# Fused two-layer block on one core: one activation table set named ahead of three norms, and two residual updates kept in PSUM

## The reference, cut to what matters

```
def rmsnorm(x, g):
    return x * lax.rsqrt(jnp.mean(x * x, axis=-1, keepdims=True) + EPS) * g

mix = (g_ssd * y_ssd + g_sc * y_sc) @ w_o                 # o1
x = x + gt1 * rmsnorm(mix, mix_post_g)                    # residual update 1
h = rmsnorm(x, ffn_pre_g) * (1.0 + sc2) + sh2             # feeds w_up (up1)
f = (silu(u_gate) * u_val) @ w_down                       # down1
x = x + gt2 * rmsnorm(f, ffn_post_g)                      # residual update 2
# layer 2
h = rmsnorm(x, attn_norm) * (1.0 + scale_a) + shift_a     # feeds w_in_2 (tok2)
...
x = x + gate_a * ((g_a * o_a + g_b * o_b) @ w_o)          # o2
h = rms_norm(x, ffn_norm) * (1.0 + scale_f) + shift_f     # feeds w_up_2 (up2)
x = x + gate_f * ((silu(gt) * val) @ w_down)              # down2
```

## Time and profile before

| | |
|---|---|
| time, median of 3 runs | 1058.37 us (1056.8 to 1060.44) |
| span of the profiled execution | 1056.5 us |
| PE busy | 1025.1 us, 97% of the span |
| ACT busy | 634.4 us, 60% |
| DVE busy | 556.2 us, 53% |
| POOL busy | 689.8 us, 65% |
| table loads of the preload (L1384) | 5, 1283 ns each |
| table loads between Ln and Exp (L1146) | 5, 1283 ns each |

### The profile page before, as it was taken

How to read it: one execution, slowest core, us unless ns; L and a number is a source line. 1 busy time by engine, 2 the same in 40 slices (tenths; PEclk the granted TensorE clock), 3 DMA queues, 4 the chain that set the end, 5 groups by cost and what they waited for, 6 DMA issues and landing times.

```text
span 1056.5 us, 23232 instructions
## 1 busy us (share of the span) xinstructions
PE 1025.1 (97%) x8537; PEld 966.4 (91%) x8537; DVE 556.2 (53%) x1165; ACT 634.4 (60%) x1133; POOL 689.8 (65%) x306
## 2 busy tenths in 40 slices
PE   7999999999999989999999899999989999999998
PEld 5999999988799979999999799998667699999998
DVE  2577625579874435565522542296566735444400
ACT  4555764477774576666645656744566557666642
POOL 2598899811269855988799287790031075988795
PEclk9999999999999999999999999999999999999999
DMA  9988888655547863777687289865201043665563
GB/s 380 383 306 282 273 307 298 235 191 187 174 146 259 282 236 105 273 235 248 204 279 268 80 283 360 330 239 191 99 21 60 1 140 122 217 193 189 168 217 111
DMA packets 62616, 226.43 MB, mean 214 GB/s; under 512 B 6960, under 2 KB 8272, under 8 KB 61264
## 3 DMA queue, kind: packets, MB, share of 16 engines
q1 hardware_dynamic: 61344, 221.23, 60.5%
q10 hardware_dynamic: 1200, 4.23, 1.4%
HBM read 224.35 MB, written 1.08 MB: 213 GB/s over the span
## 4 chain that ended last, share of the span: by engine, by line
PE 75%; issue 9%; POOL 9%; DVE 3%; ACT 3%; DMA 1%; POOLq 0%; ACTq 0%; DVEq 0%; SPq 0%
PE psL L553 68%; POOL WL L505 8%; PE psO L553 3%; PE psS L553 2%; PE psL L1092 1%; DMA ring<-wts 1%; ACT psL L1685 0%; ACT WH L1155 0%; ACT R L1273 0%; PE psS L1036 0%; ACT L1146 0%; DVE sm L2288 0%; PE psS L1063 0%; PE psS L966 0%; DVE CT L2052 0%
## 5 line engine op out<-in xcount | busy, mean ns | idle before, releaser
L505 POOL TENSOR_TENSOR WL<-ring,WH 128x1024 fp32r<-128x1024 f32 (+1 forms) x282 | 670.4, 2399 | 239.8 <-ACT WH L1155 186.7
L553 PE MATMUL psL<-HR,WH 128*128 128x256 f32 (+1 forms) x3096 | 513.5, 278 | 1.8 <-DVE HR L1796 0.9
L553 PEld LDWEIGHTS psL<-HR,WH 128*128 128x128 f32 (+1 forms) x3096 | 452.6, 187 | 7.5 <-issue 4.8
L553 PE MATMUL psL<-HR,WL 128*128 128x256 f32 x1536 | 396.2, 276 | 0.0
L1155 ACT ACTIVATE WH<-ring 128x1024 fp32r<-128x1024 f32 (+1 forms) x210 | 216.5, 1042 | 107.8 <-PE psL L553 71.9
L553 PEld LDWEIGHTS psL<-HR,WL 128*128 128x128 f32 x1536 | 275.2, 188 | 0.0
L553 PE MATMUL psL<-RR,WH 128*128 128x256 f32 x1356 | 205.2, 277 | 2.4 <-DVE RR L1981 1.2
L553 PEld LDWEIGHTS psL<-RR,WH 128*128 128x128 f32 x1356 | 185.5, 187 | 3.8 <-issue 2.8
L553 PE MATMUL psL<-RR,WL 128*128 128x256 f32 x672 | 145.0, 277 | 0.3 <-POOL WL L505 0.3
L2080 DVE SCALAR_TENSOR_TENSOR CT<-psL,par,CT 128x254 f32<-128x254 f32 (+1 forms) x176 | 80.9, 480 | 107.1 <-ACT CT L1463 102.0
L1454 ACT ACTIVATE WH<-ring 128x1024 fp32r<-128x1024 f32 (+1 forms) x88 | 92.9, 1058 | 71.4 <-PE psL L553 68.0
(11 more groups left out here) (274 smaller groups left out, 1122.8 us busy)
## 6 DMA issues: line engine op xcount, KB each, us to landing
ring<-wts SPq DMA_DIRECT2D x285, 512.0 KB, 4.2
adaring<-ada_w SPq DMA_DIRECT2D x80, 512.0 KB, 4.8
R<-ada_w SPq DMA_DIRECT2D x8, 1024.0 KB, 16.2
ring<-wts SPq DMA_DIRECT2D x16, 384.0 KB, 3.8
R<-cum_dram ACTq DMA_DIRECT2D x8, 512.0 KB, 4.1
R<-wts SPq DMA_DIRECT2D x8, 512.0 KB, 6.4
ring<-wts SPq DMA_DIRECT2D x8, 288.0 KB, 2.8
adaring<-wts SPq DMA_DIRECT2D x4, 512.0 KB, 5.2
```

What stands on the lines that cost most here:

```text
L505: nc.gpsimd.tensor_tensor(WL[:, k, 0:n], ring[:, k, 0:n], WH[:, k, 0:n].bitcast(F32), SUB).then_inc(lo_done, 1)
L553: return nc.tensor.matmul(out, lhsT, rhs, start=start, stop=stop)
```

## The change

`preload` and its five calls go. In their place `roots_table` names one set, `natural_log_exp_and_others`, three times: at the beginning of `scale_and_square` for o1 and for down1, and in the o2 stage at m == 0, behind the first `feed`. The first root of o1 and of down1 is made by `root_in_bank`: Ln goes to `RS` as before, Exp goes back into the bank `psS` from which Ln read. `add_normed` reads the root from that bank and puts the product into a free bank of `psL`, not into `CT`; it gives the bank `psS` free itself at the end. The second roots, and the one after o2, stay as they were, in `RS`.

```
-            def preload():
-
-                st.link(A(sm[:, 94:95], eps_col[:, :], ACT.Ln))
+            def roots_table():
+
+                nc.scalar.preload_act_table_set("natural_log_exp_and_others")
+
+            def root_in_bank(name):
+
+                act.wait_ge(s_done, SCRATCH[name] + 1)
+                st.link(A(RS[:, 0, :], sbank(name)[:, 0:T], ACT.Ln, scale=1.0 / D, bias=eps_col[:, :]))
+                A(sbank(name)[:, 0:T], RS[:, 0, :], ACT.Exp, scale=-0.5).then_inc(rs_ready, 1)
...
                 act.wait_ge(lead_ready, 1)
+                roots_table()
                 for m in range(8):
...
-                    if m == 6:
-                        preload()
...
             def square_x(base, sq_free_after):
 
-                preload()
...
             scale_and_square("o1", MIX, lead[:, 8:16], 0, SQ_O1)
-            stat_root("stat_o1", D, RS[:, 0, :])
+            root_in_bank("stat_o1")
...
             scale_and_square("down1", FO, lead[:, 24:32], 1, SQ_DOWN1)
-            stat_root("stat_down1", D, RS[:, 0, :])
+            root_in_bank("stat_down1")
...
                 square_o2(m)
-                if m == 6:
-                    preload()
+                if m == 0:
+                    roots_table()
...
-            def add_normed(src, rs, x_base):
-
-                def wide(buf, j, n):
-                    return buf[:, j:j + n, :]
-
-                for j, n, slot in ((0, 2, 0), (2, 2, 2), (4, 2, 0), (6, 1, 2), (7, 1, 3)):
-                    t = CT[:, slot:slot + n, :]
+            def add_normed(src, name, u0, x_base):
+
+                rs = sbank(name)[:, 0:T]
+                for i, (j, n) in enumerate(((0, 2), (2, 2), (4, 2), (6, 1), (7, 1))):
+                    t = psL[:, (u0 + 2 + i % 2) % 4, 0:n * T].rearrange("p (a b) -> p a b", b=T)
                     if j >= 4:
-                        dve.wait_ge(x_ready, x_base + j - 2)
-                    st.link(V.tensor_tensor(t, wide(src, j, n), rs.unsqueeze(1).to_broadcast([P, n, T]), MUL))
-                    V.tensor_tensor(wide(X, j, n), wide(X, j, n), t, ADD).then_inc(x_ready, n)
+                        dve.wait_ge(x_ready, x_base + j - (2 if n == 2 or j == 6 else 1))
+                    st.link(V.tensor_tensor(t, src[:, j:j + n, :], rs.unsqueeze(1).to_broadcast([P, n, T]), MUL))
+                    V.tensor_tensor(X[:, j:j + n, :], X[:, j:j + n, :], t, ADD).then_inc(x_ready, n)
+                dve.wait_ge(x_ready, x_base + 8)
+                dve.sem_inc(s_free[SCRATCH[name] % 2], 1)
...
-            add_normed(MIX, RS[:, 0, :], 0)
-            dve.wait_ge(x_ready, 8)
+            add_normed(MIX, "stat_o1", PLAN.at["up1"][1], 0)
...
-            add_normed(FO, RS[:, 0, :], 8)
...
-            dve.wait_ge(x_ready, 16)
+            add_normed(FO, "stat_down1", PLAN.at["tok2"][1], 8)
```

## The result

The changed kernel takes 1052.08 us (median of 4 runs, 1050.98 to 1054.07), the kernel before beside it 1059.12 (4 runs, 1056.8 to 1060.44): ratio 0.994, 95% interval 0.9924 to 0.9956, so 7.0 us faster. The forecast took 6.88 off. The profiled execution took 1054.07 us with a span of 1052.3.

What follows compares the result with a forecast made beforehand. PE was taken to bound the kernel, with ACT's loads counting only in the three norms. 3.41 + 3.40 - 0.56 + 0.63 = 6.88 us off the median 1058.37 gave 1051.5, range 1048.5 to 1055.0.

Steps and rivals of the forecast that it cites:

- o1 to up1: Norm after o1: early load 0.74, first Exp 1.28, DVE's wait for POOL 0.11, second Exp 1.28; gain 3.41 us.
- second Exp with `make_h`: Second root after o1: without its table load Exp comes 1.28 us earlier, and POOL doesn't hold make_h; gain 1.28.
- down1 to tok2: Norm after down1: first Exp 1.28, POOL's wait 0.16, second Exp 1.28, clock 0.68; gain 3.40 us.
- the clock: Sums in down1's norm: one PE idle stretch goes, so the clock stays up; gain 0.68 us, other end 0.
- The loads at down1: Load at down1's beginning delays POOL's split, so PE stands once; cost 0.56 us, between 0 and 1.28.
- o2 to up2: Norm after o2: Exp 1.28 earlier, but POOL's split holds make_h, whose root stays in SBUF; gain 0.63 us.
- rival (3): POOL doesn't hold make_h after o2 and down1 has slack for the load: gain 8.09, 1050.3 us; chance 0.10.
- PSUM operands: DVE operations of the first two norms: cost taken as nothing, 0.16 us at most; 0.78 by the Trainium skill.
- Rival (4): PSUM operands dearer than the 256-wide rows say, by 0.07 each: gain 6.04, 1052.3 us; chance 0.10.
- (5): Layer 2's projections, 635 to 712 us, give back the first two stages' gain: only 0.63 left, 1057.7; chance 0.12.
- (6): The named set isn't honoured and each Ln and Exp gets its own load: 3.4 slower, 1061.8 us; chance 0.05.
- a longer stretch there: Sign that the forecast is wrong: the stretch from 600 to 870 us becomes longer.

Runs made afterwards that it cites:

- before_again: The kernel before, unchanged, run once more for a second profile; 1057.76 us.
- tables_only: Against the kernel before: only the named set replaces the old preloads, roots and products stay in SBUF; 1056.95 us, ratio 0.9972.
- psum_only: Against the changed kernel: the old dummy Ln preloads put back, root and product kept in PSUM; 1057.94 us, ratio 0.9988.
- root_only: Against the changed kernel: the product goes back to CT in SBUF, only the root stays in PSUM; 1054.81 us, one run.
- load_moved: Against the changed kernel: down1's table load placed after unit 4 instead of at the stage's beginning; 1052.49 us, ratio 0.9942.
- two_loads_again: Against the changed kernel: a second table load in front of the one at down1; repetition of the same program's first run; 1053.59 us.
- last_bank: Against the changed kernel: the root after o2 also put into its PSUM bank, read there by make_h; 1051.82 us, ratio 0.9929.
- both: Against the changed kernel: down1's load after unit 4 and the root after o2 in its PSUM bank; 1050.65 us, ratio 0.9926.

## Why the prediction was right

The range held, and its steps can be read off one by one. Milestones count from PE's first `fill` matmul (381.23 and 578.05 before, 380.64 and 576.28 after), in us:

| | before, o1 | after | gain | before, down1 | after | gain |
|---|---|---|---|---|---|---|
| first Ln | 2.78 | 2.03 | 0.75 | 2.15 | 2.04 | 0.11 |
| first Exp | 4.55 | 2.52 | 2.03 | 3.92 | 2.53 | 1.39 |
| first product of DVE | 5.05 | 3.00 | 2.05 | 4.37 | 2.95 | 1.42 |
| second Ln | 12.27 | 10.11 | 2.16 | 12.32 | 10.07 | 2.25 |
| first product of the next stage | 16.19 | 12.67 | 3.52 | 16.44 | 12.82 | 3.62 |

- **o1 to up1, forecast 3.41, measured 3.52.** Early load 0.74 (0.75); first Exp 1.28 (2.03 - 0.75); DVE's wait for POOL 0.11 (2.16 - 2.05); second Exp with `make_h` 1.28, measured 1.36. Of the last 0.08, 0.07 lies between the starts of the second Exp and of `make_h`: 0.52 or 0.53 us in `before`, `before_again` and `tables_only`, 0.45 in `psum_only`, `root_only` and the changed kernel. So it comes with the new `add_normed` and not with the loads; why isn't shown.
- **down1 to tok2, forecast 3.40, measured 3.62.** First Exp 1.28 (1.39 - 0.11); POOL's wait and the clock 0.16 + 0.68 = 0.84, measured 2.25 - 1.42 = 0.83; second Exp 1.28, measured 1.37. Ln came 0.11 early, which the sum had at nothing; in `before_again` it came at 580.08 - 578.06 = 2.02, as in the changed kernel, so this belongs to the wait for a transfer in the one profile of before.
- **The loads at down1, forecast 0.56, measured 0.71.** The mechanism is right: the load sits between ACT's wait and the split on which PE depends, and `load_moved` and `two_loads_again` show that it is all of the pause. The product was forecast for 10.20 us behind PE's first of down1, and 524.00 - 513.80 is 10.20; it came 0.59 late instead of 0.56. What the sum left out is PE's slower start behind the pause, 0.11. The recorded pause, 0.43, understates the cost.
- **o2 to up2, forecast 0.63, measured 0.64**, with the other half held by POOL; `last_bank` gets it, 0.67. So rival (3) holds nowhere.
- **PSUM operands, taken at nothing.** The product takes 0.70 for 512 columns against 0.684 before, so the small bound from the earlier trace rows was near. Twelve operations at 0.065 each, the sum by the errata of the Trainium skill (VectorE: DVE Perf Modes, The TRN2 errata), would show as 0.75 for each of them; this trace has 0.70 and 0.69. Rival (4) falls.
- **DVE beside POOL.** The rule of the Trainium skill (SBUF — State Buffer, SBUF: two separate sides) is borne out: 2.08 with both inputs in SBUF, 0.70 with the root in PSUM, and `root_only` moves the wait to the addition. These are measurements of this kernel's operations; which of the two engines is held when DVE is first was not tried.
- **The clock, forecast 0.68.** Against the profile that I had, it came as said. As a reason it is weaker: the fall comes in some executions of the old norms only. In before_again there was none, yet that stage took 16.05, since DVE's first product was recorded for 1.28 there (POOL split until 583.02) and not for 0.85:

```profile
582.29 1.28 DVE L2052 TENSOR_TENSOR CT<-R,RS 128x512 f32<-128x512 f32 x1 [1.82 <-ACT RS L1146]
```

That operation ends 0.30 later than in the first profile, and the clock gives back 0.68. With that profile as the base, the gain of this stage would be 16.05 - 12.82 = 3.23 instead of 3.62, and that of all three 39.24 - 38.83 = 0.41 less.
- **Rivals (5) and (6).** From tok2 to the end of o2 it is 272.04 and 271.89 us in the two profiles of before and 273.84 and 273.29 in those of after, 1.3 to 2.0 longer. The prediction named a longer stretch there as a sign that it is wrong, and in these profiles the sign is there. But no wait takes the place of the loads. The view by stretches, before and then after:

```profile
594.50:866.50 272.00, 264.88 (x2025) 232.16 (x2026) 154.45 (x321) 159.79 (x409) 123.91 (x53) 0.99 0.47 165
```

```profile
589.10:862.90 273.80, 267.92 (x2025) 235.18 (x2026) 154.34 (x321) 159.60 (x409) 124.35 (x53) 0.99 0.47 165
```

PE stands for 7.12 us before and 5.88 after (5.35 and 5.68 in the repeated profiles); the same 2025 matmuls take 3.04 us more. Nor does the longer stretch go with the short norms: `psum_only`, with long ones, has 273.79, `both` and `two_loads_again`, with short ones, 270.07 and 270.86. What sets PE's pace in an execution stays open. The named set is honoured: Ln, Exp, Square, Identity and Copy of a stage run behind it without a load.

**How good the agreement is.** The terms measured make 3.52 + 3.62 + 0.64 - 0.71 = 7.07 against 6.88: 0.34 more in the three stages and 0.15 less at down1. That the medians, 7.0, come so near is partly luck, since the interval of the ratio goes from 4.7 to 8.0 us and since the clock behind down1, 0.68 of the sum, falls in some executions of the kernel before only.

**What the span doesn't show.** The first profile's span fell by only 4.2 us, though its stages and the load at down1 make 7.07. The view by stretches of down1, of the changed kernel in its first and then its repeated profile, at a granted clock of 1.00 in each:

```profile
528.80:543.80 15.00, 15.00 (x130) 15.00 (x129) 5.99 (x8) 7.88 (x11) 14.38 (x7) 1.00 0.85 276
```

```profile
528.80:543.80 15.00, 15.00 (x135) 15.00 (x134) 5.83 (x8) 7.36 (x10) 14.47 (x7) 1.00 0.87 282
```

PE never stands, but does 130 matmuls where it otherwise does 134 or 135. up1 and down1 took 182.97 us in the first profile and 181.03 in the repeated one, 180.63 before; the stretch to o2, above, has the same scatter. It belongs to an execution and not to the change: `last_bank`, too, took 276.81 in layer 2 and `both`, with the same edit, 270.07. A single run of the kernel before beside the repeated profiles took 1065.63 us, 5.2 above the slowest of the four above. So 4.2 of one pair of spans is no measure, and the medians' 7.0 agrees with the stages' 7.07.

## What to carry to other kernels

An activation table load between two dependent functions is worth its length only where its consumer can use the time: look at what runs beside the consumer at the new, earlier moment, here POOL's split: with the loads alone the stages and down1 win 3.6 us of 7.1 (39.24 - 34.95 - 0.71). Take DVE off that path by giving each operation one input in PSUM. A load that is moved ahead must be weighed as an added instruction in ACT's order, at the one place where a split behind it is late; in the middle of down1 it cost nothing, at its head 0.71, of which the recorded pause shows 0.43. And compare stages, not spans, when the change is under a per cent: the stages repeated to 0.03 us where the spans scattered by several.

## What the hardware showed beside this

PE's pace varies at a granted clock of 1.00: three matmuls of a step take 0.340 us in most places and 0.353 in patches of some executions, almost 4% more, with PE busy throughout and no wait. And one execution, the first of `two_loads`, ran 3182.07 us, 75 matmuls in 30 us where at the pace of the view above about 270 fit:

```profile
1500.00:1530.00 30.00, 30.00 (x75) 30.00 (x75) 4.21 (x9) 5.12 (x8) 7.08 (x3) 1.00 0.22 70
```

The same kernel then took 1053.59. The page of this execution has no row of the granted clock, as the pages of all the others have, so the 1.00 in this view is no measurement, and a throttled clock isn't excluded. What slowed it, the profile doesn't name; the cause stays open, as does that of the patches.
